# Gate rows and conv tiles by seven block products for eight, in a new order of the front, in a Trainium2 hybrid-layer kernel

## The reference, cut to what matters

```
h    = rms_norm(x) * gain
proj = h @ w_in      # columns: hq 512, hf 512, hi 512, hg 512, gqkv 1536, gz 512, ga 4, gb 4
f    = lb + (1 - lb) * sigmoid(hf);  k = 1 - f;  log f is summed up along a chunk
hi: the values of the HGRN2 heads;  silu(hg), silu(gz): the output gates of both head groups
qkv  = silu(causal_conv4(gqkv));  gq, gk normalised; decays and beta from ga, gb
per chunk:  K K^T and Q K^T, times decays; a unit triangular system is inverted; then a scan over the chunks
mixed @ w_out, a gated MLP with a causal convolution of width 3, a per-layer embedding   # not touched
```

## Time and profile before

| what | value |
|---|---|
| median of 3 runs (1424.33 to 1425.36) | 1424.34 us |
| span of the profiled execution, first to last instruction | 1422.4 us |
| PE busy | 1410.8 us, 99% |
| DVE busy | 1027.0 us, 72% |
| ACT busy | 705.3 us, 50% |
| POOL busy | 221.3 us, 16% |
| mean granted clock of PE | 0.999 of full speed |

### The profile page before, as it was taken

How to read it: one execution, slowest core, us unless ns; L and a number is a source line. 1 busy time by engine, 2 the same in 40 slices (tenths; PEclk the granted TensorE clock), 3 DMA queues, 4 the chain that set the end, 5 groups by cost and what they waited for, 6 DMA issues and landing times.

```text
span 1422.4 us, 19769 instructions
## 1 busy us (share of the span) xinstructions
PE 1410.8 (99%) x7235; PEld 1187.2 (83%) x7235; DVE 1027.0 (72%) x1522; ACT 705.3 (50%) x1309; POOL 221.3 (16%) x239
## 2 busy tenths in 40 slices
PE   9999999999999999999999999999999999999998
PEld 7877888888889999888888888888888888888886
DVE  7594545561149887368988999999999576577567
ACT  6443456422258887258663443343345444454455
POOL 4000001101038785010000000000000245300000
PEclk9999999999999999999999999999999999999999
DMA  9442424545623342545442334334327755424213
GB/s 277 68 74 30 45 82 122 148 111 121 152 82 100 118 119 83 207 133 186 126 126 82 119 122 145 114 109 149 119 89 250 247 191 194 139 82 134 89 60 148
DMA packets 153247, 181.00 MB, mean 127 GB/s; under 512 B 21241, under 2 KB 92095, under 8 KB 153152
## 3 DMA queue, kind: packets, MB, share of 16 engines
q1 hardware_dynamic: 153152, 179.74, 43.1%
HBM read 130.43 MB, written 49.28 MB: 126 GB/s over the span
## 4 chain that ended last, share of the span: by engine, by line
PE 94%; DVE 3%; ACT 2%; issue 1%; DMA 0%; DVEq 0%; SPq 0%; ACTq 0%
PE psum L2456 9%; PE psum L2457 9%; PE psum L2458 9%; PE psum L2395 5%; PE psum L2397 5%; PE psum L2396 5%; PE psum L1373 4%; PE psum L674 4%; PE psum L676 4%; PE psum L675 4%; PE psum L2368 4%; PE psum L2369 4%; PE psum L2370 4%; PE psum L734 3%; PE psum L732 3%; PE psum L733 3%
## 5 line engine op out<-in xcount | busy, mean ns | idle before, releaser
L166 DVE TENSOR_TENSOR w_wlo<-w_raw,w_whi 128x1024 fp32r<-128x1024 f32 x66 | 87.4, 1325 | 228.3 <-ACT w_whi L151 228.2
L151 ACT ACTIVATE w_whi<-w_raw 128x1024 fp32r<-128x1024 f32 x66 | 69.7, 1058 | 175.1 <-PE psum L2370 77.1
L3189 DVE TENSOR_TENSOR g_slot<-w_raw,g_slot 128x512 fp32r<-128x512 f32 x77 | 67.6, 878 | 59.1 <-ACT g_slot L2763 59.1
L674 PE MATMUL psum<-h_hi,w_whi 128*128 128x512 f32 x256 | 100.7, 393 | 0.0
L2763 ACT ACTIVATE g_slot<-w_raw 128x512 fp32r<-128x512 f32 x77 | 48.7, 632 | 104.8 <-PE psum L2397 99.7
L676 PE MATMUL psum<-h_hi,w_wlo 128*128 128x512 f32 x256 | 99.8, 390 | 0.0
L675 PE MATMUL psum<-h_lo,w_whi 128*128 128x512 f32 x256 | 99.7, 390 | 0.0
L3447 POOL TENSOR_TENSOR mixed_home<-mixed_home 128x512 f32<-128x512 f32 x11 | 14.7, 1339 | 508.3 <-DMA mixed_home<-in_w_down 505.0
L2368 PE MATMUL psum<-w_whi,m_hi 128*128 128x512 f32 x224 | 87.8, 392 | 0.0
L2370 PE MATMUL psum<-w_whi,m_lo 128*128 128x512 f32 x224 | 87.2, 389 | 0.0
L2369 PE MATMUL psum<-w_wlo,m_hi 128*128 128x512 f32 x224 | 87.2, 389 | 0.0
(11 more groups left out here) (446 smaller groups left out, 3995.8 us busy)
## 6 DMA issues: line engine op xcount, KB each, us to landing
w_raw<-in_w_up SPq DMA_DIRECT2D x39, 512.0 KB, 3.9
w_raw<-in_w_in SPq DMA_DIRECT2D x36, 512.0 KB, 6.7
s_rows<-pair_work SPq DMA_DIRECT2D x11, 1024.0 KB, 4.1
w_raw<-s_rows SPq DMA_DIRECT2D x44, 256.0 KB, 2.6
g_rows<-pair_work SPq DMA_DIRECT2D x18, 512.0 KB, 2.6
w_raw<-g_rows SPq DMA_DIRECT2D x33, 256.0 KB, 3.4
w_raw<-in_w_out SPq DMA_DIRECT2D x16, 512.0 KB, 4.4
mixed_home<-in_w_down SPq DMA_DIRECT2D x32, 256.0 KB, 3.5
```

Of the source, the lines that this page charges most:

```text
L674: pe.matmul(out, wh[:, w], self.hi[:, kt, part], start=(kt == 0), stop=False)
```

## The change

The products of the conv tiles and of the gate rows go through seven block products for eight (Winograd's form of Strassen's scheme, with 512 x 512 blocks). `Pieces` is new: 28 row pieces (7 steps of 4) and 42 pair pieces (6 pairs of conv tiles, 7 steps each), a piece being 12 products with 128 x 512 weights per rounded half. The weight sums are made by POOL in place (`row_sums`: 16, `pair_sums`: 24 operations of 128 x 512). The four sums of h are made by DVE (`dve_form`: 8 operations of 128 x 2048), rounded by ACT (`act_sum`), with their remainders by DVE (`dve_sum_lo`: 4 of 128 x 2048). One sum takes the place of a quarter of h, which is saved to memory and loaded again for f and q. The running sums of the scheme stay in PSUM: a bank is copied out by ACT or joined by DVE, and the next step adds to it. The ring has four homes; a piece is rounded three pieces ahead.

The order of PE becomes: values (in place of the first conv tiles, while x is turned), the gates' small product, gate rows, pairs, f with all eight chunks, q with the first inverse. What is removed: 48 products of the rows and 72 of the conv tiles. Conv: the first tap is ACT's (`act_tap`), three stay on DVE (`dve_taps`); the square moves from DVE to ACT. A chunk sits in every slot from 1 to 8, its turn in the next; a slot is now 12 products, with the turn after the first six and the chunk after the last six (K K and Q K ahead of the spread). Scaling V moves from ACT to DVE. ACT loads the Exp table ahead of each slot, and Sigmoid's in every second slot. The steps of the first inverse move to the heads 2 and 3 of q; the inversion of the blocks moves behind the chunks.

```diff
+class Pieces:
+    RING, AHEAD, PAIRS, QUAD = 4, 3, 3 * NH // 2, KT // 2
+    STEPS = 7
+    B11, B21, T2, T3, T1, B22, T4 = range(STEPS)
+    ROWS = STEPS * QUAD
+        self.order = [(0, self.B11)]
+        for p in range(self.PAIRS):
+            self.order += [(p, q) for q in (self.B21, self.T2, self.T3, self.T1)]
+            if p + 1 < self.PAIRS:
+                self.order.append((p + 1, self.B11))
+            self.order += [(p, self.B22), (p, self.T4)]
...
+    def row_sums(self, pool):
+        b = self.row_block
+        for kt in range(self.QUAD):
+            pool.wait_ge(self.rest, kt + 1)
+            self.row_landed(pool, 1, 0)
+            pool.tensor_tensor(b(0, 0, kt), b(1, 0, kt), b(0, 0, kt), ALU.subtract).then_inc(self.made, 1)
+        pool.wait_ge(self.slabs.rest, self.slabs.QUADS)
...
+    def round(self, act, n):
...
+        self.multiplied.wait(act, ("front_piece", n - self.RING) if n >= self.RING else ("slab", 1 - n // 2))
+        act.activation(self.home(n)[0], self.source(n), ACT.Copy).then_inc(self.rounded, 1)
+
+    def remainder(self, dve, n):
...
+        dve.wait_ge(self.rounded, n + 1)
+        dve.tensor_tensor(lo, self.source(n), hi.bitcast(F32), ALU.subtract).then_inc(self.rest, 1)
...
 class Front:
-    SPREAD = (0, 2, 3, 5, 6, 8, 9, 11)
+    SPREAD = tuple(range(1, NT + 1))
+    F_UNITS = ((0, 1), (1, 1), (0, 0), (1, 0), (2, 1), (3, 1), (2, 0), (3, 0))
+    SLOTS = 2 * len(F_UNITS)
+    ROUNDED_AT = {5: 2, 7: 3, 13: 4}
...
     def pe(self, pe):
...
+        for n in range(pc.ROWS):
+            self.pe_row_piece(pe, n)
+        for p, q in pc.order:
+            if q == pc.B22 and 0 < 2 * p - 1 < 2 * NH:
+                self.pe_sum(pe, 2 * p - 1)
+            if q == pc.T2 and 0 <= 2 * p - 4 < 2 * NH:
+                self.pe_sum(pe, 2 * p - 4)
+            if (p, q) == (pc.PAIRS - 1, pc.B22):
+                self.pe_len_columns(pe)
+                self.pe_cumulate(pe)
+            self.pe_pair(pe, p, q)
+        for i, (h, half) in enumerate(self.F_UNITS):
+            if i == 2:
+                pe.wait_ge(s["saved"], 4 * 16)
+            for two in range(KT // 2):
+                self.pe_turned(pe, "f", h, half, i % 4, half == 0, range(2 * two, 2 * two + 2))
+                slot, late = divmod(4 * i + two, 2)
+                for c in range(NT):
+                    if late and self.SPREAD[c] == slot:
+                        self.pe_chunk(pe, c)
+                    if not late and self.SPREAD[c] + 1 == slot:
+                        self.pe_chunk_turn(pe, c)
         for h in range(NH):
             for half in range(2):
-                if h in (1, 2):
-                    self.scan.pe_first_inverse(pe, 2 * (h - 1) + half)
+                if h >= 2:
+                    self.scan.pe_first_inverse(pe, 2 * (h - 2) + half)
...
     def act(self, act):
+            elif q == pc.B22:
+                if p:
+                    self.act_square_hi(act, 2 * p - 2)
+                if p == last:
+                    self.act_factors(act)
+            elif q == pc.T4:
+                self.act_pair_line(act, p)
+                self.act_tap(act, 2 * p + 1)
+        slabs.round(act, self.first["f"], m_)
+        self.act_silu(act, 2 * last + 1)
+        self.act_tap(act, 2 * last)
+        slabs.round(act, self.first["f"] + 1, m_)
+        self.act_silu(act, 2 * last)
+        k.table(act, ACT.Exp)
+        for slot in range(self.SLOTS):
+            self.act_slot(act, slot)
+            if slot % 2:
+                h, half = self.F_UNITS[slot // 2]
...
+                if slot + 1 < self.SLOTS:
+                    self.banks.released(act, key)
+                    k.table(act, ACT.Exp)
+            if slot in self.ROUNDED_AT:
+                slabs.round(act, first["f"] + self.ROUNDED_AT[slot], m_)
...
     def dve(self, dve):
+        for n in range(pc.ROWS):
+            pc.remainder(dve, n + pc.AHEAD)
+            if n < 2:
+                self.dve_form(dve, 7 + n)
+            elif n < 6:
+                self.dve_sum_lo(dve, (self.S2, self.S3, self.S1, self.S4)[n - 2])
...
+            elif q == pc.T3 and p:
+                self.dve_taps(dve, 2 * p - 2)
+            elif q == pc.T1:
+                self.dve_pair_join(dve, p, pc.B21)
+                if p:
+                    self.dve_square_lo(dve, 2 * p - 1)
...
+            elif q == pc.T4:
+                self.dve_taps(dve, 2 * p + 1)
+        slabs.remainder(dve, self.first["f"])
+        self.dve_pair_join(dve, last, pc.T4)
+        slabs.remainder(dve, self.first["f"] + 1)
+        self.dve_taps(dve, 2 * last)
+        for slot in range(self.SLOTS - 5):
+            self.dve_slot(dve, slot)
+            if slot in (5, 7):
+                self.dve_open(dve, (slot - 5) // 2)
+            if slot in self.ROUNDED_AT:
+                slabs.remainder(dve, first["f"] + self.ROUNDED_AT[slot])
+        dve.wait_ge(s["queried"], NT)
...
+        self.dve_solve(dve)
+        slabs.remainder(dve, first["q"] + 2)
...
     def dve_slot(self, dve, slot):
...
+                self.multiplied.wait(dve, ("a_scores", c))
...
+                self.multiplied.wait(dve, ("a_turn", c))
+                beta = small[:, 7, c, :].unsqueeze(2).broadcast_to([P, NH, P])
+                self.banks.release(dve.tensor_tensor(self.chunk(2, c), heads(self.banks.of(("a_v", c))), beta, ALU.mult), ("a_v", c))
...
     def dve_solve(self, dve):
         for i in range(SB - 1):
-            if i % 12 == 11:
-                next_slab()
+            if i == 4:
+                slabs.remainder(dve, first["q"])
+            elif i == 7:
+                self.dve_open(dve, 2)
+            elif i == 12:
+                self.dve_open(dve, 3)
+            elif i == 15:
+                slabs.remainder(dve, first["q"] + 1)
...
     def sp(self, sp):
+        for c in range(NT):
+            self.sp_chunk(sp, c)
+            if c in (3, 5):
+                self.slabs.load(sp, first["q"] + 1 + (c == 5))
+        sp.wait_ge(s["lt_stored"], NT * 16)
```

More of the change, by code:

```diff
@@ new lines, in sp @@
+        sp.wait_ge(s["squared"], NT)
+        for m in (0, 1, 3):
+            tile(m)
+        self.sp_rows(sp, pc.B21, 0, 4)
+        self.sp_rows(sp, pc.T3, 1, 0)
+        for t in range(4):
+            self.banks.released(sp, ("front_rows", pc.T3, t))
+        tile(2)
+        self.sp_rows(sp, pc.B22, 1, 4)
+        self.sp_rows(sp, pc.T4, 0, 0)
+        for m in range(4, 3 * NH):
+            tile(m)
+        last = pc.PAIRS - 1
+        sp.wait_ge(pc.rest, pc.number(last - 1, pc.T4) + 1)
@@ L652, in pe_quad @@
             for at in range(2):
                 kt = 2 * j + at
[L654 to L659 removed]
+                wh, wl = self.slabs.halves(j, at * DG, DG)
@@ L660, in pe_quad @@
+                pe.matmul(out, self.hi[:, kt, part], wh, start=(j == begins and at == 0), stop=False)
+                pe.matmul(out, self.hi[:, kt, part], wl, start=False, stop=False)
+                ins = pe.matmul(out, self.lo[:, kt, part], wh, start=False, stop=(kt == KT - 1))
+            keys = [key] if j == ends else []
+            if half == 1 and t == t1 - 1:
                 keys.append(("slab", j))
@@ new lines, in act_row_out, with act_pair_copy @@
+    def act_row_out(self, act):
+        for t in range(4):
+            key = ("front_rows", self.pieces.B22, t)
+            self.multiplied.wait(act, key)
+            act.wait_ge(self.stored[t], 4 * 16)
+            self.banks.release(act.activation(self.rstage[t][:], self.banks.of(key), ACT.Silu), key)
+    def act_pair_copy(self, act, p, q, tile, joined):
+        key = ("pairs", p, q)
+        self.multiplied.wait(act, key)
+        if p:
+            self.banks.released(act, ("pairs", p - 1, joined))
+        self.banks.release(act.activation(tile[:], self.banks.of(key), ACT.Copy), key)
@@ L778, in act @@
+    def act_square_hi(self, act, m):
+        if m >= 2 * NH:
+            return
+        at = self.place(m)
+        act.wait_ge(self.s["sq"], at + 1)
+        if at:
+            self.multiplied.wait(act, ("sum", self.place(at - 1)))
+        else:
+            for i in range(self.STAGES):
+                act.wait_ge(self.stored[i], 6 * 16)
+        act.activation(self.sqhi[:], self.sq[:], ACT.Copy).then_inc(self.s["sq_hi"], 1)
     def act(self, act):
-        k, s, slabs, m_ = self.k, self.s, self.slabs, self.multiplied
+        k, s, slabs, m_, pc = self.k, self.s, self.slabs, self.multiplied, self.pieces
@@ L836, in act @@
-        self.act_chain(act)
-        self.act_silu(act, 3 * NH - 1)
-        z, small = self.z, self.small
-        act.activation(small[:, 7], self.gcol[:, :, NH:2 * NH], ACT.Sigmoid).then_inc(s["act"], 1)
+        pc.round(act, 0)
+        pc.round(act, 1)
+        self.act_sum(act, self.S1)
+        pc.round(act, 2)
+        act.wait_ge(slabs.rest, 3)
+        for half in range(2):
+            key = ("gates", half)
+            m_.wait(act, key)
```

(5 more changed lines are left out.)

994 lines of the change are left out of this document (626 added, 368 removed).

## The result

The kernel after takes 1483.9 us (median of four runs) against 1424.3: a ratio of 1.042, 95% interval 1.040 to 1.043. The forecast was slower, 1446, with a range of 1411 to 1464. The sign was right, the size 38 us short, and the time lies 20 us above the range.

What follows compares the result with a forecast made beforehand. The prediction took PE's queue of products, busy for 99% of the span, as the bound. Waits of 49.5 us less 27.7 saved gave plus 21.8 on 1422.4, with 1.9 around it 1446 us, slower; range 1411 to 1464.

Steps and rivals of the forecast that it cites:

- products out of PE's queue: Gate rows and conv tiles: 48 and 72 products fewer, with half-width ones made full, 27.7 us less.
- rows, POOL beside DVE: First seven row pieces: POOL's sums and DVE's operations partly in turn, a wait of 3 us (0 to 13).
- pairs: Six conv-tile pairs: DVE and POOL work partly in series, 2 us of PE waits (0 to 8).
- f's start: Ahead of f: PE waits for the first slab's remainder behind factors, table loads and taps, 6.7 us.
- turns: Chunks' turns of V and K: each of eight waits 1.2 us, the first also for Exp's table; 10.6 in all.
- slots 5 and 7: Chunk slots: table loads and remainders delay DVE (5.9 us), SP's slab loads delay the chunks' stores (3.0); 8.9.
- q and the inverse: Heads of q: first product with the inverse waits 9.7 us, three late slabs bring it to 14.8.
- the scan's start: First scan products: DVE's preparation comes late behind x's stores and two slabs, 2 us (0 to 5).
- clock: PE after a long wait: some products at half rate, 1.5 us (0 to 4).
- The chain of latencies behind the last turn: From the last chunk's turn: inversion starts at 9.5 us, ends at 43.4, inverse loaded at 59.7 to 63.2.
- The rival with the lock in full: Rows and pairs: DVE and POOL go strictly in turn, waits 13 and 8 us, 1462 us; chance 0.12.
- faster: Rival: path from last pair to inverse one sixth shorter, waits under 24.9 us, faster by over 2.8; chance 0.28.

Runs made afterwards that it cites:

- e4: Kernel after with POOL's weight sums (all in the rows, three of four per pair) cut to 8 columns, leaving out work the result needs: 1468.9 us.
- e5: Kernel after with the row sum of squares in the pairs moved from ahead of B22 to ahead of T4: 1489.7 us.
- e10: Kernel after with ACT's copy of T1's bank ahead of a silu and the sum of squares ahead of T4: 1479.0 us.
- e6: Kernel after with f's first slab rounded ahead of the factors, its remainder and the last join ahead of the last pair's taps: 1483.2 us.
- e1: Kernel after with the spread ahead of K K and Q K in every chunk: 1479.4 us.
- e2: Kernel after with SP loading q's slabs 1 and 2 behind chunks 4 and 6 instead of 3 and 5: 1471.2 us.
- e8: Kernel after with e1, e2, e5, e6, f's slabs 2 and 3 in slots 6 and 8, loads behind chunks 5 and 7, later slabs in the inversion: 1461.9 us.
- e13: Kernel after with SP loading lt and x once x's own stores have landed, without waiting for xt's: 1479.0 us.
- e3: Kernel after with 126 useless PE products filling its long waits, from f's start to the inverse: 1478.9 us.
- e9: Kernel after with ACT's copy of T1's bank ahead of a silu, the sum of squares staying ahead of B22: 1485.1 us.
- e12: Kernel after with e1, e6, e10, re-timed slab loads and rounding, plus 46 useless products in chunk 0's turn and ahead of the inverse: 1444.1 us.

## Why the prediction was short by 38 us

Term by term, us:

| step of the prediction | said | measured | seen in |
|---|---|---|---|
| products out of PE's queue | -27.7 | taken as said | counts of 336 and 504, 0.227 apart |
| rows, POOL beside DVE | 3 | 6.6 (4.6 to 6.6 in the runs that keep this stage) | e4 |
| pairs | 2 | 14.0 | e4, e5, e10 |
| f's start | 6.7 | 6.4 | e6 |
| turns | 10.6 | 8.0 | e1 |
| slots 5 and 7 | 8.9 | 18.6 | e2, e8 |
| q and the inverse | 14.8 | 10.9 | e13 |
| the scan's start | 2 | 1.8 | the waits |
| clock | 1.5 | 22.9 (with some 4 of ends) | e3, the windows |

Two sums of the prediction are off by themselves: 22.4 against 20.9 in six pairs is 0 to 9 and not 8, and the turns' 9.4 and 1.0 make 10.4 and not 10.6. Neither matters for the error.

**What held.** The chain of latencies behind the last turn did almost to the microsecond: that turn ends at 393.7, the inversion begins 8.4 later (said 9.5), ends 43.4 later (43.4) and its first product runs 60.0 later (59.7 to 63.2). The last step of it is partly luck: POOL's cut took 2.1 for 1.26, the stores of both cuts had landed 9.0 behind their first issue for 10.4 at the quickest, the loads 5.3 behind theirs for 4.4. The turns wait 1.0 each (1.2); only the first table was not late. f's remainder ended 13.6 behind T1 (13.4). One path runs from f's start to the inverse, and e1 and e6 show what that means: what is gained at its beginning is waited for at its end.

**The clock: 1.5 for 22.9.** This is the largest error and the step that failed first: a mis-sized term. The row of the kernel's end showed that the clock falls; I priced one wait of 10 us. PE had 33 waits for 7 before, four of them of 6 us and more, and the windows show a low clock behind each of these and behind some of the 2 us waits. Not all of the 22.9 is clock: the profile counts a product 0.39 long where the next starts 0.227 later, so each wait leaves 0.16 more of busy time, some 4 us in all. And e3 gave back only 8.6 us of busy time at the places that it filled. How the rest divides no run shows; an estimate from windows of 1 us (busy time times what the granted clock lacks to 1.00) gives 3.1 in the rows, 1.7 in the pairs, 6.8 from f's start to 395 us and 6.0 behind, 17.5 in all, which with the 4 comes near the 22.9.

Slow products and waits can also stand for each other. In the rows PE gets its remainder every 4.97 us whatever its clock: the waits there were 1.96, 0.76, 1.95 and 1.96 in the kernel after and 1.96, 0.36, 1.94 and 0.36 in e9, at the same distances. As long as DVE set the pace there, the lost clock cost nothing more.

**The pairs: 2 for 14.0.** Two steps failed. DVE's and POOL's times of one pair were set in series, 22.4 against 20.9, and then only 2 of the 8 were taken; the trace has three taps in 4.95 for 3.93 where a sum of POOL meets them, and e4 halves the squares' wait. And ACT's silu ahead of the copy of T1 was not in my list at all: a wait that the profile of the kernel after doesn't name either, since another stands at the same place. It took two edits at once to show it.

**The rows: 3 for 6.6.** I held that the two engines "met only now and then in the rows" of before, and took 3 of 13. In this order they meet all the time. With the clock behind those waits, and the share in the pairs, POOL's sums and their lock cost 15.0 (e4). The rival with the lock in full had 13 and 8 us for the two places and the trace has 6.6 and 14.0; near as the sums are, this is partly luck, since only 5.5 of the pairs' 14.0 went with POOL's sums.

**Slots 5 and 7: 8.9 for 18.6.** The queue was right: stores behind a load behind a remainder. I priced the store at its landing time of before, 2.4, but behind 512 KB it took 8.8: 13.4 us of waits for 3.0. The remainder's own delay gave the waits of 3.6, 2.6 above a plain turn, as e2 leaves them: 5.2 for 5.9.

**The side that was 3.9 too high.** q's slab 2 came in time, and the wait for the inverse was 8.1 for 9.7, as PE was itself held up before it.

So of the rivals, "faster" needed a path one sixth shorter than the 146 us of its rows. From the last pair's T1 to the first product with the inverse it took 162.7: 43.9 of waits, where the terms had 41, and 118.8 of work for 105, most of the difference being slow products by the estimate above.

## What to carry to other kernels

Taking products out of a full queue pays only with what feeds it in hand: price a new wait with the slow products that can stand behind it, not by its length alone. A place in a queue is also a transfer's place: with a 512 KB load ahead of it a 256 KB store landed after 8.8 us for 2.4, and moving the load one chunk later gained more than any other single edit that keeps the result (12.7 us). When removing a wait makes a kernel slower, look for the second one that it hid; and test edits on one path together too, since alone some of them seem to do nothing.

## What the runs showed that I had not expected

DVE and POOL, once both always have work with two operands from SBUF, settle in turns for some 20 us: a round of two DVE operations (0.69 and 2.28 alone) and two POOL sums (1.29 each) took 4.98, near their sum of 5.55 and far from the 2.97 of DVE alone. Small POOL operations pay too: of e4's four last sums of 8 columns in the rows three took 2.18 us beside DVE's 2.28, and the one beside an idle DVE 0.20.

A wait of 2.5 us is followed by a low clock in some executions and not in others: behind the same wait (2.49 us until 197.1) the kernel after shows

```profile
196.00:200.00 4.00, 2.88 (x13) 2.05 (x14) 3.10 (x4) 3.66 (x6) 1.31 (x1) 1.00 0.86 116
```

and e3, whose fillers come only later, behind 2.47 us until 195.2

```profile
196.00:200.00 4.00, 4.00 (x13) 2.97 (x11) 2.39 (x3) 2.25 (x4) 1.12 (x1) 0.64 1.01 141
```

It may be why kernels with many short waits scatter over several us (1440.6 to 1449.1 in e12) where the kernel before stays within 1.0 to 3.5; no run here tests it.
